# A hybrid decoder block on one core: the last store of the gate matrix, some row gathers and the first expert group's gate in another order

## Chip, cores and metric

One Trainium2 chip, one core. The metric is the device time of one execution in microseconds (us); the median of several runs is compared. Engines: PE is the matmul engine (TensorE), DVE is VectorE, ACT is ScalarE, POOL is GpSimd, SP is the engine that issues most transfers (DMAs).

## The reference, cut to what matters

One decoder block on 512 tokens of width 2048: pooling and latent attention, then a product-key expert layer, then a gated embedding. The change lies in the expert layer:

```python
def peer_ffn(xn, wq, sub_keys, u, v):
    q = (xt @ wq).reshape(t, PEER_HEADS, 2, PEER_HALF_DIM)
    sc = jnp.einsum('thpc,hpnc->thpn', q, sub_keys)
    top_v, top_i = lax.top_k(sc, PEER_TOPK)
    ...                                  # 16 best of the 256 pairs, for each of 8 heads
    gate = jax.nn.softmax(best_v, axis=-1)
    hc = jnp.einsum('cd,chkd->chk', xc, u[ec])      # u, v: 16384 x 2048
    ac = gc * jax.nn.gelu(hc)
    out = jnp.einsum('chk,chkd->cd', ac, v[ec])
```

## The kernel before

Tokens lie along the free axis, features along the partitions. Every weight unit (16 blocks of 128 by 128) is loaded as two halves of 512 KB into `raw`, split by ACT into a rounded part `w_hi` (`hi`, L1155) and by DVE into the rest `w_lo` (`lo`, L1643), and multiplied by PE in three passes of 16 blocks, 48 matmuls in a unit. `raw` is one buffer of two halves: a half is loaded again only when its `lo` is done (`load_unit`, L509).

The expert layer computes 342 of the 512 tokens densely, against all 16384 experts, with a gate matrix (expert by token) that is zero but for the chosen pairs. The other 170 tokens are done row by row: POOL gathers one row of u or v for each of 128 partitions (1 MB, `load_row`, L2483), DVE multiplies and sums it (L2045).

Before the groups the gate matrix is made in DRAM. For the first 128 dense tokens POOL scatters single gates (`put_gate_of`: 8 heads with 16 puts each; the first put of a head waits until all puts of the heads before have landed). For the other tokens DVE makes one-hot vectors in 27 sets, PE multiplies them, ACT evicts them into `g_blk` and SP stores seven blocks; of the last one (L583, 256 KB) the part that the first groups need goes first and the remaining 1792 KB follow (L604). While this runs, PE computes u units that are spilled, and DVE takes ten `early_row` dots at fixed places between the sets; with two buffers, the gather of an early row waits for the dot two rows before. POOL issues the gathers of early rows 2 to 9 between the sixteen puts of the last head: two puts, one gather, and so on (L2531 to L2534).

Then come 32 groups of 4 times 128 experts. A group is three u units (k = 0 to 2) and four v units (k = 3 to 6). The gate path of one of its four blocks is a chain of small instructions: DVE `scale`, ACT `gelu`, DVE `gate`, ACT `gated_hi`, DVE `gated_lo`. ACT's `between(k, j, a)` puts the conversion of the halves of unit k around gelu and gated_hi; DVE's `chain` does the same for `lo`. Each engine works in the order written.

Group 0 is special (`first=True`). Its units still use `raw`. SP loads the halves of k = 3, then issues `load_g` for group 1 (the gate tile, L610, and the spilled products, L613), then loads k = 4 to 6. ACT evicts the second set of token rows into `x_rows_b` (`rows_evict_b`, L1474) between k = 3 and k = 4; that tile lies over `g_blk`, so the first eviction waits until all stores of the blocks have landed:

```python
if i == 0:
    act.wait_ge(g_stored[0], 16 * ((ONE_TB + 1) // 2))      # L1477
```

Behind it on ACT stand the second eviction, two `rows_stage_b` (16 small copies), and then the conversion of k = 4. DVE's second `gated_lo` into the next group waits for the same count. POOL starts the gathers of the groups' rows when the stores and the second half of k = 3 have landed; group 0 has three rows, the later ones 10 or 11. Below, v0, v1, v2, v3 are the v units of group 0 (k = 3 to 6).

## Time and profile before

| | us |
|---|---|
| runs before: median of 3 | 2986.7 |
| lowest and highest of them | 2975.47, 2995.12 |
| the profiled execution | 2986.3 |
| its span, first to last instruction | 2984.5 |
| PE busy in the span | 2946.4 |

The profile is of one execution. 1.8 us of its time lie outside the span. A transfer's time to landing runs from its issue to the completion. The granted clock is 1.00 at full speed (2.4 GHz) and 0.50 at half (1.2 GHz).

### The profile page before, as it was taken

Reading aid. Unit: us, or ns where it says so; the run is one execution under the profiler, and the core shown is the slowest. Engines: PE = TensorE matmul, PEld = TensorE weight load, DVE = VectorE, ACT = ScalarE, POOL = GpSimd, SP = SyncE. Lnnn points to the kernel's source line nnn. Section 1 sums busy time; section 2 is a strip of 40 time slices with the busy share of each in tenths; the row PEclk is TensorE's granted clock in tenths of the full one; section 3 lists DMA queues with packets and bytes.
Section 4 is the critical chain, followed back from the end, with each engine's and each line's share of the span. In section 5 each row is a group of like instructions: output and inputs, shape, how many; then the busy total and the mean of one; then the engine's idle time right before and its main releaser. Section 6 shows DMA issues by size and latency. Waiting matters only on the chain.

```text
span 2984.5 us, 45570 instructions
## 1 busy us (share of the span) xinstructions
PE 2946.4 (99%) x17422; PEld 2746.1 (92%) x17422; DVE 2459.3 (82%) x3694; ACT 1057.9 (35%) x1433; POOL 775.4 (26%) x519
## 2 busy tenths in 40 slices
PE   9999999999999999999999999999999999999998
PEld 7777778888999999999999999999999999999887
DVE  7544443479998969999999999999999999998745
ACT  5224332232234653323333333333333333334522
POOL 0120000027776202222222222323333333230000
PEclk9999999999999999999999999999999999999999
DMA  4242222345557889999999999999999999995322
GB/s 170 91 160 98 84 71 98 112 121 143 144 125 220 301 289 361 349 357 382 360 376 359 364 385 365 375 375 367 373 367 377 359 370 372 372 366 184 107 98 100
DMA packets 209496, 779.52 MB, mean 261 GB/s; under 512 B 50561, under 2 KB 104065, under 8 KB 135041
## 3 DMA queue, kind: packets, MB, share of 16 engines
q1 hardware_dynamic: 136784, 413.90, 38.3%
q0 software_dynamic: 67680, 358.71, 33.0%
q10 hardware_dynamic: 4944, 5.81, 0.6%
q8 instruction: 47, 0.77, 0.1%
q14 instruction: 41, 0.33, 0.0%
HBM read 745.22 MB, written 33.10 MB: 261 GB/s over the span
## 4 chain that ended last, share of the span: by engine, by line
PE 75%; DVE 13%; DMA 4%; SPq 3%; issue 3%; POOL 1%; ACT 1%; DVEq 0%; ACTq 0%; POOLq 0%
PE bank L656 23%; PE bank L657 23%; PE bank L658 23%; DVE w_lo L1656 2%; DMA raw_whole<-in_u_t 2%; SPq L613 2%; DVE row L2045 2%; POOL gate_matrix L2478 1%; PE bank L747 1%; DVE w_lo L1643 1%; PE bank L770 1%; PE bank L748 1%; DVE h L2231 1%; DMA raw_whole<-in_v_t 1%; DVE one_g L2093 1%
## 5 line engine op out<-in xcount | busy, mean ns | idle before, releaser
L656 PE MATMUL bank<-x_hi,w_hi 128*128 128x342 f32 (+2 forms) x2912 | 1001.1, 344 | 11.6 <-DVE w_lo L1643 5.0
L657 PE MATMUL bank<-x_lo,w_hi 128*128 128x342 f32 (+2 forms) x2912 | 997.3, 342 | 0.0
L658 PE MATMUL bank<-x_hi,w_lo 128*128 128x342 f32 (+2 forms) x2912 | 991.0, 340 | 0.0
L656 PE MATMUL bank<-a_hi,w_hi 128*128 128x342 f32 x2048 | 654.1, 319 | 7.1 <-DVE a_lo L2146 2.5
L658 PE MATMUL bank<-a_hi,w_lo 128*128 128x342 f32 x2048 | 652.0, 318 | 0.0
L657 PE MATMUL bank<-a_lo,w_hi 128*128 128x342 f32 x2048 | 649.7, 317 | 0.0
L656 PEld LDWEIGHTS bank<-x_hi,w_hi 128*128 128x128 f32 x2912 | 549.6, 189 | 54.5 <-DVE w_lo L1656 6.7
L657 PEld LDWEIGHTS bank<-x_lo,w_hi 128*128 128x128 f32 x2912 | 548.3, 188 | 37.1 <-issue 1.2
L658 PEld LDWEIGHTS bank<-x_hi,w_lo 128*128 128x128 f32 x2912 | 548.4, 188 | 37.0
L656 PEld LDWEIGHTS bank<-a_hi,w_hi 128*128 128x128 f32 x2048 | 387.0, 189 | 14.8 <-issue 9.2
L657 PEld LDWEIGHTS bank<-a_lo,w_hi 128*128 128x128 f32 x2048 | 387.3, 189 | 0.0
L658 PEld LDWEIGHTS bank<-a_hi,w_lo 128*128 128x128 f32 x2048 | 386.8, 189 | 0.0
L1175 ACT ACTIVATE w_hi<-raw_whole 128x1024 fp32r<-128x1024 f32 x216 | 223.0, 1053 | 452.0 <-DMA raw_whole<-in_u_t 196.6
L1175 ACT ACTIVATE w_hi<-raw_b_whole 128x1024 fp32r<-128x1024 f32 x216 | 223.0, 1053 | 443.4 <-DMA raw_b_whole<-in_u_t 187.6
L2497 POOL DMA_INDIRECT row<-in_v,expert x128 | 205.6, 1607 | 478.3 <-DVE x_rows L2058 286.8
L2478 POOL DMA_INDIRECT gate_matrix<-put_gate,cell x128 | 233.9, 1827 | 338.2 <-DVE cell L1982 289.8
L1643 DVE TENSOR_TENSOR w_lo<-raw_whole,w_hi 128x1024 fp32r<-128x1024 f32 (+1 forms) x218 | 256.8, 1204 | 64.5 <-ACT w_hi L1162 60.9
L2058 DVE SCALAR_TENSOR_TENSOR x_rows<-row,mix,x_rows 128x2048 f32<-128x2048 f32 x127 | 297.6, 2343 | 0.0
L2497 POOL DMA_INDIRECT row<-in_u_rows,expert x113 | 152.5, 1349 | 519.3 <-DVE row L2045 456.7
L1656 DVE TENSOR_TENSOR w_lo<-raw_whole,w_hi 128x1024 fp32r<-128x1024 f32 x216 | 263.2, 1219 | 23.9 <-ACT w_hi L1175 23.8
L1656 DVE TENSOR_TENSOR w_lo<-raw_b_whole,w_hi 128x1024 fp32r<-128x1024 f32 x216 | 263.1, 1218 | 19.4 <-ACT w_hi L1175 19.4
L1162 ACT ACTIVATE w_hi<-raw_whole 128x1024 fp32r<-128x1024 f32 (+1 forms) x218 | 217.5, 1030 | 172.5 <-PE bank L658 51.6
(271 smaller groups left out, 3174.2 us busy)
## 6 DMA issues: line engine op xcount, KB each, us to landing
raw_whole<-in_v_t SPq DMA_DIRECT2D x62, 1024.0 KB, 7.6
raw_b_whole<-in_v_t SPq DMA_DIRECT2D x62, 1024.0 KB, 8.1
raw_b_whole<-in_u_t SPq DMA_DIRECT2D x46, 1024.0 KB, 9.2
raw_whole<-in_u_t SPq DMA_DIRECT2D x46, 1024.0 KB, 8.8
raw_whole<-in_u_t SPq DMA_DIRECT2D x72, 512.0 KB, 4.1
beside<-gate_matrix SPq DMA_DIRECT2D x31, 704.0 KB, 15.4
raw_whole<-in_w_o SPq DMA_DIRECT2D x32, 512.0 KB, 3.9
raw_whole<-in_w_q SPq DMA_DIRECT2D x32, 512.0 KB, 3.8
```

The source lines that it names most:

```text
L613: sp.dma_start(h_pre[par][:, :, :], by_quarters(h_dram[g])).then_inc(h_in[par], 16)
L656: pe.matmul(out, w_hi[slot][:, blk, :], m_hi, start=first, stop=False)
L657: pe.matmul(out, w_hi[slot][:, blk, :], m_lo, start=False, stop=False)
L658: return pe.matmul(out, w_lo[slot][:, blk, :], m_hi, start=False, stop=last)
L1162: act.activation(w_hi[slot][:, 8 * s:8 * s + n, :], raw[s][:, 0:n, :], ACT.Copy)\
L1175: act.activation(w_hi[slot][:, 8 * s:8 * s + 8, :], raw_two[x][s][:, :, :], ACT.Copy).then_inc(hi_ready, 1)
L1643: dve.tensor_tensor(w_lo[slot][:, 8 * s:8 * s + n, :], raw[s][:, 0:n, :], w_hi[slot][:, 8 * s:8 * s + n, :].bitcast(F32), ALU.subtract)\
L1656: dve.tensor_tensor(w_lo[slot][:, 8 * s:8 * s + 8, :], raw_two[x][s][:, :, :], w_hi[slot][:, 8 * s:8 * s + 8, :].bitcast(F32), ALU.subtrac ...
L2045: dve.scalar_tensor_tensor(got[:, :], got[:, :], 1.0, (x_rows_b if part_b else x_rows)[:, :], ALU.mult, ALU.mult, accum_out=column(dots_b ...
L2058: dve.scalar_tensor_tensor(to[:, :], row[b][:, :], column(mix_b if part_b else mix, k), to[:, :], ALU.mult, ALU.add).then_inc(row_done, 1)
L2478: pool.indirect_dma_start(g_dram.rearrange("b j i t -> (b j i t)").unsqueeze(1), bass.IndirectOffsetOnAxis(ap=cell[:, hd, k:k + 1], axis=0 ...
L2497: pool.indirect_dma_start(into[:, :], None, table, bass.IndirectOffsetOnAxis(ap=index, axis=0))\
```

## The change

Four edits. (1) On SP the rest of the last block is no longer stored before the waits ahead of group 0 but inside group 0, behind the loads of v0 and `load_g` for group 1. (2) On ACT and DVE, in group 0 only, the gate of block p+2 is done whole before v0 is converted, instead of around it. (3) On POOL the gathers of group 0 and 1 get waits of their own: row 0 for v0's second half (as before), row 1 for v1's first half, row 2 for all stores and v1's second half, group 1's first row for v2's first half. (4) On POOL the gathers of early rows 2 and 3 go ahead of the last head's first puts; of its puts, 12 then stand between the gathers and 4 behind the last.

```diff
--- before.py
+++ after.py
@@ -601,7 +601,6 @@
             for b in range(stored, ONE_TB):
                 store_block(b, b % 2)
             load_unit(U_PEER + 3, packed(u_t, GROUP))
-            sp.dma_start(g_dram[N_TB - 1, :, TOPK:NK, :], g_blk[(ONE_TB - 1) % 2][:, TOPK:NK, :]).then_inc(g_stored[0], 16)
             sp.wait_ge(g_stored[1], 16 * (ONE_TB // 2))
             sp.wait_ge(g_first, 16)
             sp.wait_ge(spill_stored, 16 * N_GROUPS)
@@ -627,6 +626,9 @@
                         sp.dma_start(pt[:, :, :], p_t).then_inc(p_in, 16)
                     if first and q == 0:
                         load_g(g + 1, 1 - par)
+                    if first and q == 0:
+                        sp.dma_start(g_dram[N_TB - 1, :, TOPK:NK, :], g_blk[(ONE_TB - 1) % 2][:, TOPK:NK, :])\
+                            .then_inc(g_stored[0], 16)
 
             peer_group(0, 0, first=True)
             sp.wait_ge(g_stored[0], 16 * ((ONE_TB + 1) // 2))
@@ -1533,7 +1535,11 @@
                 if last:
                     activate(p + 2, a_slot(2, par))
                 else:
-                    between(3, p + 2, a_slot(2, par))
+                    if first:
+                        activate(p + 2, a_slot(2, par))
+                        hi_peer(g, 3, par, first=True)
+                    else:
+                        between(3, p + 2, a_slot(2, par))
                     if first:
                         rows_evict_b(0)
                         rows_evict_b(1)
@@ -2210,6 +2216,14 @@
                     scale(p + 2, 2, par, g2, peer_unit(g, 1), (2 + par) % 2)
                     gate(p + 2, 2, par, g2)
                     gated_lo(p + 2, 2, par)
+                elif first:
+                    scale(p + 2, 2, par, g2, peer_unit(g, 1), (2 + par) % 2)
+                    gate(p + 2, 2, par, g2)
+                    gated_lo(p + 2, 2, par)
+                    rows(3)
+                    lo_half(3, 0)
+                    lo_half(3, 1)
+                    rows(4)
                 else:
                     chain(p + 2, 2, par, g2, 3, 3, peer_unit(g, 1), (2 + par) % 2)
                     rows(4)
@@ -2506,6 +2520,16 @@
                     else:
                         k = first_b(g) + b_places(g).index(n)
                         index = expert_b[:, k:k + 1]
+                    if g == 0 and n == 0:
+                        pool.wait_ge(raw_loaded[1], 16 * (peer_unit(0, 3) + 1))
+                    if g == 0 and n == 1:
+                        pool.wait_ge(raw_loaded[0], 16 * (peer_unit(0, 4) + 1))
+                    if g == 0 and n == 2:
+                        for s in range(2):
+                            pool.wait_ge(g_stored[s], 16 * ((ONE_TB + 1 - s) // 2))
+                        pool.wait_ge(raw_loaded[1], 16 * (peer_unit(0, 4) + 1))
+                    if g == 1 and n == 0:
+                        pool.wait_ge(raw_loaded[0], 16 * (peer_unit(0, 5) + 1))
                     load_row(first_place(g) + n, index, table)
 
             pool.wait_ge(zeros_stored, 16 * 2 * PUT_TB)
@@ -2528,18 +2552,17 @@
                         load_row(TOP)
                     if hd == PH - 2 and k == TOPK // 2 + 2:
                         load_row(TOP + 1)
-            for k in range(2, EARLY):
+            load_row(TOP + 2)
+            load_row(TOP + 3)
+            for k in range(4, EARLY):
                 for j in range(2):
-                    put_gate_of(PH - 1, 2 * k - 4 + j)
+                    put_gate_of(PH - 1, 2 * k - 8 + j)
                 load_row(TOP + k)
-            for k in range(2 * EARLY - 4, TOPK):
+            for k in range(2 * EARLY - 8, TOPK):
                 put_gate_of(PH - 1, k)
             pool.wait_ge(row_done, FRONT)
             pool.wait_ge(g_done, 2 * N_OH)
-            for s in range(2):
-                pool.wait_ge(g_stored[s], 16 * ((ONE_TB + 1 - s) // 2))
             pool.wait_ge(expert_b_in, 16 * 2 * SHARE)
-            pool.wait_ge(raw_loaded[1], 16 * (peer_unit(0, 3) + 1))
             for g in range(G_DOT):
                 load_group(g, u_rows)
             for g in range(G_DOT, N_GROUPS - 1):
```

## Rows read from the trace of the kernel before

**Rows 1.** The page: engines over the span, and the group of the puts.

```profile
PE 2946.4 (99%) x17422; PEld 2746.1 (92%) x17422; DVE 2459.3 (82%) x3694; ACT 1057.9 (35%) x1433; POOL 775.4 (26%) x519
...
L2478 POOL DMA_INDIRECT gate_matrix<-put_gate,cell x128 | 233.9, 1827 | 338.2 <-DVE cell L1982 289.8
```

**Rows 2.** Windows: PE, PEld, DVE, ACT, POOL busy (x instructions), clock, DMA share, GB/s.

```profile
1000.00:1062.00 62.00, 61.95 (x587) 59.87 (x585) 59.11 (x70) 41.93 (x46) 7.44 (x4) 1.00 0.74 275
...
1171.00:1330.00 159.00, 153.65 (x970) 151.14 (x969) 147.20 (x180) 52.35 (x66) 43.05 (x31) 1.00 0.95 360
1913.00:1966.00 53.00, 53.00 (x341) 52.95 (x340) 52.31 (x52) 17.62 (x22) 18.23 (x11) 1.00 0.98 375
```

**Rows 3.** Waits of PE in 925 to 1000 us: us in total, times, longest.

```profile
PE bank L656 <- DVE x_lo L1643: 2.2, 2, 1.8
PE bank L949 <- DVE one_g L2093: 1.7, 2, 0.9
PE bank L949 <- ACT g_blk L1436: 0.4, 1, 0.4
PE bank L656 <- DVE w_lo L1643: 0.3, 1, 0.3
```

**Rows 4.** The chain of waits, 918 to 938 us (start us, us, what).

```profile
918.97 6.20 DMA gate_matrix<-put_gate,cell
...
929.99 7.99 DMA early_row<-in_u_rows,expert
```

**Rows 5.** Timeline of DVE, the same stretch (start us, us, what, idle before).

```profile
930.93 1.23 DVE L1643 TENSOR_TENSOR x_lo<-raw_whole,x_hi 128x1024 fp32r<-128x1024 f32 x1 [0.32 <-ACT x_hi L1162]
938.00 2.29 DVE L2045 SCALAR_TENSOR_TENSOR early_row<-early_row,x_rows 128x2048 f32<-128x2048 f32 x1 [5.84 <-DMA early_row<-in_u_rows,expert]
```

**Rows 6.** Transfers, five stretches: count, KB each, median us to landing.

```profile
raw_whole<-in_u_t SPq DMA_DIRECT2D x3, 512.0 KB, 3.4
...
raw_whole<-in_u_t SPq DMA_DIRECT2D x1, 512.0 KB, 7.3
...
gate_matrix<-g_blk SPq DMA_DIRECT2D x1, 2048.0 KB, 8.9
...
gate_matrix<-g_blk SPq DMA_DIRECT2D x1, 1792.0 KB, 10.2
...
beside<-spilled_scores SPq DMA_DIRECT2D x1, 176.0 KB, 8.3
```

**Rows 7.** Timeline of the SP queue around group 0.

```profile
1071.67 0.43 SPq L604 DMA_DIRECT2D gate_matrix<-g_blk  x1
...
1081.34 0.44 SPq L610 DMA_DIRECT2D beside<-gate_matrix  x1
1081.82 0.65 SPq L613 DMA_DIRECT2D beside<-spilled_scores  x1
```

**Rows 8.** Wait of PE in 1080 to 1120 us (as rows 3).

```profile
PE bank L656 <- DVE a_lo L2146: 2.5, 1, 2.5
```

**Rows 9.** Timeline of ACT in group 0.

```profile
1088.85 1.07 ACT L1479 ACTIVATE x_rows_b<-bank 128x512 f32<-128x512 f32 x2
...
1093.62 1.05 ACT L1162 ACTIVATE w_hi<-raw_whole 128x1024 fp32r<-128x1024 f32 x1
1094.57 0.49 ACT L1483 ACTIVATE beside<-h_s 128x352 f32<-128x352 f32 x1
```

**Rows 10.** Windows in group 0 (columns as rows 2).

```profile
1091.00:1096.00 5.00, 5.00 (x24) 5.00 (x23) 1.30 (x2) 4.06 (x14) 1.81 (x2) 0.66 0.91 328
1096.00:1103.00 7.00, 6.58 (x46) 6.35 (x45) 4.22 (x8) 2.53 (x4) 0.00 (x0) 1.00 1.01 401
```

**Rows 11.** The chain of waits into the third v unit.

```profile
1107.62 1.07 ACT w_hi L1162
...
1108.71 1.24 DVE w_lo L1643
...
1110.04 0.39 PE bank L656
```

## Prediction

> **What bounds the kernel now.** I read the page first: PE is busy 99% of the span [rows 1], so an edit pays only by idle or half-clock time of PE that it removes, and costs only what it adds of these. The windows over the expert groups say how much there is. A full group window of 53 us holds 341 matmuls, 0.155 us each, so a unit of 48 takes 7.5 us. Groups 1 to 3 hold 970 in 159 us where 1023 would fit: 53 are missing, 8.2 us, and the transfers are busy 95% of that time [rows 2]. So PE is the bound in late groups, and any shift of PE's work before them reaches the end, unless these 8.2 us of stalls change with it.
>
> Then I asked for PE's waits around the two places that the diff touches. Between 925 and 1000 us PE waits 4.6 us in six pieces, nearly all for DVE [rows 3]. The chain of waits tells what held DVE: POOL's put waits 6.2 us for the puts of the heads before, then come two puts, then an early row's gather takes 8.0 us [rows 4], and DVE stands still for 5.84 us before that row's dot [rows 5]. After 1000 us, with DVE busy for 59.1 of 62 us, PE is busy for 61.95: no stall is left there [rows 2]. In group 0 PE waits 2.5 us for `a_lo`, the gate of block p+2 [rows 8]; a little later its clock is at the lower level, 1.2 GHz, for a time: 0.66 of full speed over 5 us, 1.7 us lost [rows 10].
>
> **Edit 4, early rows 2 and 3 ahead of the puts.** The put that waits at 918.97 for 6.2 us is the first of the last head; in that time POOL does nothing. The gather of early row 2 needs only a dot that is done, so it is issued about 922, after the put that starts at 918.97, and not at 929.99; with the same 8.0 us it lands at 930, before DVE comes to it at 932.1 [rows 4, 5]. DVE's 5.84 us of idling would go. What may take their place is the half that DVE splits just before, at 930.93, whose conversion it waited for by 0.32 us [rows 5]. Halves of this stretch land in 3.4 us; one that ran beside a gather and puts took 7.3 [rows 6]. Now two gathers (2.1 MB) run beside it. Ends: not slowed, 5.84 us of lead for DVE; slowed by 3.9 us, some 2 us of lead. I take a half of about 5 us, 1.6 late, and 4.3 us of lead, since the two gathers share the transfer engines with little else. The stalls are 4.6 us in all [rows 3] and are served by the lead one after another, so the gain is the smaller of the two: **−4.3 us**, bounds −2.0 and −4.6. The later early gathers keep their waits on dots and move with DVE. Four puts, at 1.8 us each [rows 1], now follow the last gather. SP needs all puts landed only before group 0's first gate tile, some 30 us on, so they cost nothing; without that cover it would be up to 4 × 1.8 us plus the 6.2 us wait of rows 4.
>
> **Edit 2, the gate of p+2 ahead of v0.** Its work is the same, in another order: no instruction more or less. `a_lo` comes before v0's halves have landed, and what PE waits for is v0's second `w_lo`, 2.4 us after its conversion starts (1.09 + 1.24 + the start, as in [rows 11]). The wait of 2.5 us shrinks, at best to nothing; I take a shrinkage of 1.4 us, and the clock stays up. Those 1.4 + 1.7 us are gained only if v1 is ready when v0 ends. It is not, by the next step, so here I cost it at 0.
>
> **Edit 1, the store behind v0 and the gate tile.** SP issued it at 1071.67; now it comes after L613, which is issued from 1081.82 to 1082.47 [rows 7]. It adds nothing to SP's queue but its issue of 0.43 us. The wait that counts is ACT's at L1477: the first eviction into `x_rows_b`. Before, the store had landed at 1071.67 + 10.2 = 1081.9 [rows 6, 7] and the eviction ran at 1088.85 with no wait. Now it runs when the store lands; call that S. Queued behind it on ACT are the second eviction, two stagings and v1's conversion, which began 4.8 us after the first eviction [rows 9]; who waits for them is DVE's `lo` of v1 and with it PE. From the start of v1's conversion to PE's start on v1 I count 4.5 us: 1.1 to the first `lo`, 1.2 for it, 0.9 for one addition and the gate product between the two `lo` on DVE, 1.3 for the second `lo` and the start (durations from [rows 9, 11]). So v1 starts at S + 9.3.
>
> S, from below: the fastest of the block stores shown took 8.9 us from issue, although 2048 KB [rows 6]: 1082.5 + 8.9 = 1091.4. From above: what stands ahead in the queue, the spilled products, lands at 1081.82 + 8.3 = 1090.1 [rows 6, 7]; if the store's 1.84 MB and row 0's gather of 1.05 MB, which POOL issues at about 1087, then share 401 GB/s [rows 10], it is 2.89 / 0.401 = 7.2 us more: 1097.3. I take 1096.0, nearer to the upper end, because the queue is not empty as it was at 1071.67: 0.9 MB of small pieces are ahead. v1's own halves are issued from 1087 on, behind the store, and need 2.6 us of the same rate; they land before ACT comes to them at S + 4.8.
>
> The Trainium skill, DMA: Bandwidth & Descriptors, section "Queues, rings and completion order", says that each transfer engine consumes one queue in order and alternates between queues by packets. This trace agrees as far as it goes: the spilled products, issued last, land last of that set. By the rule the whole gather could be served between the store's packets, which is the upper end, 1097.3, and would make the sum 1.3 us larger.
>
> PE's side: v1 starts at 1105.3. v0 now ends near 1097, so PE idles about 8 us. An idling of 2.5 us was followed by the 1.7 us of half clock above [rows 8, 10], so I add 1.7 for this longer one. v1 takes 7.5, and v2 starts at S + 9.3 + 7.5 + 1.7 = S + 18.5 = 1114.5. Before it started at 1110.04 [rows 11]. From there on the order is as before. **Cost: S − 1091.5 = +4.5 us.** Bounds: with S at 1091.4 and no clock loss −1.8; with S at 1097.3 +5.8, and +7.5 if the half clock lasts twice as long.
>
> **Edit 3, the gathers' waits.** Row 0 goes no later than before. Rows 1 and 2 leave v1's and the store's way and land about 1108, group 1's first row about 1120. DVE multiplies the three rows at the starts of v1, v2 and v3 and the fourth in group 1, after 1125, so the slack is 5 us or more: 0. If this cover went, DVE would wait for one row, up to about 5 us.
>
> **Sum.** 2986.3 (the profiled execution) − 4.3 + 0 + 4.5 + 0 = 2986.5, span 2984.7. The median of the runs is 0.4 above the profiled execution, so 2986.9, rounded to **2987 us**.
>
> **Rivals.**
> - *The early store (faster).* S is at 1092 or less because the store's large pieces overlap the small ones ahead. Then v1 is ready when PE is nearly done with v0, edit 2's gain counts and the clock stays up: −1.8 − 4.3 = 2980.2. Against it: 0.9 MB ahead in the queue. It begins to win as S falls under 1092.
> - *The late store (slower).* S at 1097.3 and a longer half clock: +7.5 − 4.3, 2989.5, and with edit 4's lead at its lower bound 2991.8. It decides as soon as S is later than 1095.8, where edit 1 costs more than edit 4 gives. For it: transfers are busy 91 to 101% of this time [rows 10].
> - *The first groups' stalls move.* 8.2 us are lost in groups 1 to 3 for late transfers [rows 2]; another spacing of the gathers there could remove most of it: −7.5, 2979. Against it: from group 1's second row on the gathers wait for DVE's dots, in both kernels.
> - *No effect.* The half before early row 2 is as late as it can be (+2.3 against the sum), and the delay of group 0 is taken back in the groups' stalls (−4.5): about 2984.
>
> **Chances.** Forecast (2984.5 to 2989) 0.35, early store 0.15, late store 0.25, stalls move 0.15, no effect 0.10. All five lie within 8 us of the sum. The three runs of before spread over 19.7 us, so a median may be 5 us or more off. The range is 2979 to 2991.8 widened by about 4 us to each side: **2975 to 2996**. The forecast's own range is 2982 to 2992. About 1%, 30 us, is what a measurement of this kernel can tell from no change; no case reaches it. Faster by over 1% 0.02, within 1% 0.97, slower by over 1% 0.01.
>
> **What would show it.** Edit 4 is right if DVE's 5.84 us before the early row at 938 are gone and PE's six waits before 1000 with them, and group 0 starts 4 us earlier. Edit 1 is right if ACT idles before the first L1479 until the store lands, 13 to 14 us after its issue, and PE then waits about 8 us for v1's `w_lo` with the clock at half for a while. Edit 2 is right if the wait for `a_lo` is replaced by a shorter one for `w_lo`. The forecast is wrong if the store lands in under 10 us, or if the matmuls missing in groups 1 to 3 are not 50 or so again.

## The result, and the profile after

The changed kernel takes 2991.4 us (median of 22 runs, 2982.9 to 3002.5) where the kernel before takes 2984.7 on the same chips (22 runs, 2975.5 to 2995.3). The ratio is 1.0020, with a 95% interval of 1.0012 to 1.0029: slower by 0.2%, 6 us, and within 1%. The forecast was 2987 in a range of 2975 to 2996, a change of 0.2 us and within 1%. The profiled execution of the changed kernel took 2991.1 us, its span is 2989.3.

In the changed kernel's profile line numbers are 2 to 14 higher than before: the matmuls are L658 to L660, `lo` is L1649, `hi` L1164, the eviction L1481, the late store L630, `load_g` L609 and L612, a row's dot L2051, its gather L2511.

The page: the engines over the span, and the group of the puts. PE is busy for the same time as before [rows 1]; the 4.8 us that this span has more than the 2984.5 before are idling of PE.

```profile
PE 2946.3 (99%) x17422; PEld 2747.1 (92%) x17422; DVE 2459.2 (82%) x3694; ACT 1058.2 (35%) x1433; POOL 794.4 (27%) x519
...
L2492 POOL DMA_INDIRECT gate_matrix<-put_gate,cell x128 | 233.4, 1823 | 334.4 <-DVE cell L1988 289.8
```

**Edit 4, the early rows.** PE's waits from 925 to 1000 us (answer to [rows 3]) are 2.5 us instead of 4.6:

```profile
PE bank L658 <- DVE w_lo L1649: 1.3, 2, 1.0
PE bank L658 <- DVE x_lo L1649: 0.8, 1, 0.8
PE bank L951 <- ACT g_blk L1438: 0.4, 1, 0.4
```

The chain of waits and DVE's timeline of the same stretch (answers to [rows 4, 5]):

```profile
924.20 7.83 DMA raw_whole<-in_u_t
```

```profile
933.15 1.23 DVE L1649 TENSOR_TENSOR w_lo<-raw_whole,w_hi 128x1024 fp32r<-128x1024 f32 x1 [1.77 <-ACT w_hi L1164]
935.79 1.23 DVE L1649 TENSOR_TENSOR x_lo<-raw_whole,x_hi 128x1024 fp32r<-128x1024 f32 x1 [1.42 <-ACT x_hi L1164]
936.94 2.28 DVE L2051 SCALAR_TENSOR_TENSOR early_row<-early_row,x_rows 128x2048 f32<-128x2048 f32 x1
```

The early row is there in time: its dot at 936.94 has no idling ahead of it, where there were 5.84 us. But it starts only 1.1 us earlier than before (938.00), because DVE splits two halves ahead of it, waits for each (1.77 and 1.42 us), and the first of them landed 7.83 us after its issue. Group 0's gate tile is issued at 1063.12 instead of 1064.17.

**Edit 1, the store.** The queue of SP (answer to [rows 7]), ACT (answer to [rows 9]) and the chain of waits (answer to [rows 11]):

```profile
1080.69 0.43 SPq L609 DMA_DIRECT2D beside<-gate_matrix  x1
1081.17 1.13 SPq L612 DMA_DIRECT2D beside<-spilled_scores  x1
1082.34 2.49 SPq L630 DMA_DIRECT2D gate_matrix<-g_blk  x1
```

```profile
1093.54 1.09 ACT L1481 ACTIVATE x_rows_b<-bank 128x512 f32<-128x512 f32 x2 [6.62 <-DMA gate_matrix<-g_blk]
...
1098.32 1.04 ACT L1164 ACTIVATE w_hi<-raw_whole 128x1024 fp32r<-128x1024 f32 x1
```

```profile
1082.34 11.13 DMA gate_matrix<-g_blk
...
1112.20 9.66 DMA raw_whole<-in_v_t
...
1124.31 0.63 PE bank L658
```

The store is issued at 1082.34 and lands at 1093.5, the moment S of the prediction. ACT idles 6.62 us for it, and v1's conversion starts at S + 4.8. PE's waits from 1092 to 1130 us (answer to [rows 8]):

```profile
PE bank L658 <- DVE w_lo L1649: 7.9, 2, 4.3
PE bank L908 <- ACT stage_b L1429: 1.8, 2, 1.3
```

The waits come in three places: 1.8 us for `stage_b` and 3.6 us for v1's `w_lo`, both behind the eviction, and then 4.3 us, in one piece, for v3's. Ahead of them, at v0, PE waits 1.2 us for `w_lo` where it waited 2.5 us for `a_lo`, and the clock stays up (1.00 from 1087 to 1093.5, where 1091 to 1096 before had 0.66). The kernel before waits at v1 and v2 too: beside the line of [rows 8] its waits of 1080 to 1120 have a second one, 0.4 us at v1 and 1.5 us at v2.

```profile
PE bank L656 <- DVE w_lo L1643: 1.9, 2, 1.5
```

The wait for v3 is the one that the prediction had no term for. Its half is the 9.66 us of the chain above. A load of 1 MB of group 1's u, issued at 1112.65, ran beside it, and POOL's timeline shows what else did, three gathers of 1 MB:

```profile
1108.54 0.94 POOL L2511 DMA_INDIRECT row<-in_u_rows,expert  x1 [8.38 <-DMA raw_whole<-in_v_t]
1109.78 1.65 POOL L2511 DMA_INDIRECT row<-in_u_rows,expert  x1 [0.30 <-issue]
1115.49 0.94 POOL L2511 DMA_INDIRECT row<-in_u_rows,expert  x1 [4.06 <-DVE row L2051]
```

Windows of the changed kernel (columns as in [rows 2]; the last one answers a row there). The clock after each of the two idle stretches is at its lower level, and in 1072 to 1080 the transfer engines are busy for a fifth of the time:

```profile
1072.00:1080.00 8.00, 8.00 (x52) 7.99 (x52) 4.94 (x8) 4.85 (x8) 0.00 (x0) 1.00 0.21 80
```

```profile
1100.00:1107.00 7.00, 4.29 (x15) 4.32 (x16) 6.52 (x10) 2.17 (x4) 0.16 (x1) 0.51 0.96 343
1124.00:1128.00 4.00, 3.69 (x15) 3.73 (x16) 4.00 (x7) 2.01 (x2) 0.00 (x0) 0.58 0.73 242
1171.00:1330.00 159.00, 157.77 (x1005) 156.68 (x1004) 152.63 (x186) 53.19 (x66) 43.83 (x33) 1.00 0.97 371
```

The kernel before, the first of these windows:

```profile
1072.00:1080.00 8.00, 8.00 (x55) 8.00 (x54) 4.30 (x8) 5.58 (x8) 0.00 (x0) 1.00 0.89 308
```

This pair is the heart of the case. Before, the 1792 KB of the store filled a stretch in which nobody else wanted the transfer engines (share 0.89), and it had landed 7 us before ACT asked for it. After, that stretch is empty (0.21) and the store stands where v0's and v1's halves and a row's gather are wanted.

**Where the 6 us come from.** Group 0 starts 1.0 us earlier. v2 starts at 1112.3 instead of 1110.04, 2.3 us later. v3 starts at 1124.3 instead of 1117.7, 6.6 us later, and then loses some 1.6 us at the half clock (4 us at 0.58). The gate tile of group 3 is issued 8.0 us later than before (1178.09 against 1170.13), that of group 4 only 5.2 us later (1230.89 against 1225.67). From 1171 to 1330 PE does 1005 matmuls instead of 970 [rows 2]; at 0.155 us the 35 are 5.4 us, which leaves a delay of 2.6 us at 1330. The span ends 4.8 us later, so about 2 us are lost again behind it.

Whether the 5.4 us are group 0's delay taken back isn't shown. In the 160 us from 110 us after group 0's gate tile (two windows of each profile, added) the kernel before does 978 matmuls and the changed one 1013, but the twelve kernels below do 993 to 1026, those too whose group 0 isn't late (x1_early_rows 1026, x4_store_back 1016). The profiled execution of the kernel before stalls more there than any other.

### The profile page after: what moved, and what is told of

Its sections match the earlier page's. It is cut to its first block, busy times and chain, and to the rows that moved or that the text cites. A ratio compares the mean times of both kernels' runs of the same rounds, so it can differ in the third digit from the quotient of the medians.

```text
span 2989.3 us, 45570 instructions
## 1 busy us (share of the span) xinstructions
PE 2946.3 (99%) x17422; PEld 2747.1 (92%) x17422; DVE 2459.2 (82%) x3694; ACT 1058.2 (35%) x1433; POOL 794.4 (27%) x519
## 4 chain that ended last, share of the span: by engine, by line
PE 60%; DVE 23%; DMA 8%; SPq 4%; issue 3%; ACT 2%; DVEq 0%; ACTq 0%
PE bank L658 18%; PE bank L659 18%; PE bank L660 18%; DVE w_lo L1662 6%; DVE row L2051 5%; DMA raw_whole<-in_u_t 4%; SPq L612 3%; DMA raw_b_whole<-in_u_t 2%; DVE h L2245 2%; DVE w_lo L1649 1%; DVE x_rows L2064 1%; PE bank L749 1%; DMA raw_whole<-in_v_t 1%; PE bank L772 1%; PE bank L750 1%
## 5 line engine op out<-in xcount | busy, mean ns | idle before, releaser
L658 PE MATMUL bank<-x_hi,w_hi 128*128 128x342 f32 (+2 forms) x2912 | 1001.5, 344 | 13.0 <-DVE w_lo L1649 6.6
L660 PE MATMUL bank<-x_hi,w_lo 128*128 128x342 f32 (+2 forms) x2912 | 990.7, 340 | 0.0
L658 PE MATMUL bank<-a_hi,w_hi 128*128 128x342 f32 x2048 | 654.3, 319 | 11.7 <-DVE w_lo L1649 9.1
L660 PE MATMUL bank<-a_hi,w_lo 128*128 128x342 f32 x2048 | 652.6, 319 | 0.0
L658 PEld LDWEIGHTS bank<-x_hi,w_hi 128*128 128x128 f32 x2912 | 549.6, 189 | 56.5 <-DVE w_lo L1662 5.2
L660 PEld LDWEIGHTS bank<-x_hi,w_lo 128*128 128x128 f32 x2912 | 548.4, 188 | 37.2
L658 PEld LDWEIGHTS bank<-a_hi,w_hi 128*128 128x128 f32 x2048 | 387.7, 189 | 17.6 <-DVE w_lo L1649 8.6
L660 PEld LDWEIGHTS bank<-a_hi,w_lo 128*128 128x128 f32 x2048 | 387.5, 189 | 0.0
L1177 ACT ACTIVATE w_hi<-raw_b_whole 128x1024 fp32r<-128x1024 f32 x216 | 223.1, 1054 | 439.4 <-PE bank L660 197.6
L2511 POOL DMA_INDIRECT row<-in_v,expert x128 | 217.1, 1696 | 455.9 <-DVE x_rows L2064 270.7
L1649 DVE TENSOR_TENSOR w_lo<-raw_whole,w_hi 128x1024 fp32r<-128x1024 f32 (+1 forms) x218 | 256.8, 1204 | 72.8 <-ACT w_hi L1164 69.2
L2511 POOL DMA_INDIRECT row<-in_u_rows,expert x113 | 152.5, 1349 | 516.9 <-DVE row L2051 446.0
L1164 ACT ACTIVATE w_hi<-raw_whole 128x1024 fp32r<-128x1024 f32 (+1 forms) x218 | 217.4, 1030 | 170.9 <-PE bank L660 51.5
```

The source lines that it names most:

```text
L658: pe.matmul(out, w_hi[slot][:, blk, :], m_hi, start=first, stop=False)
L660: return pe.matmul(out, w_lo[slot][:, blk, :], m_hi, start=False, stop=last)
L1164: act.activation(w_hi[slot][:, 8 * s:8 * s + n, :], raw[s][:, 0:n, :], ACT.Copy)\
L1177: act.activation(w_hi[slot][:, 8 * s:8 * s + 8, :], raw_two[x][s][:, :, :], ACT.Copy).then_inc(hi_ready, 1)
L1649: dve.tensor_tensor(w_lo[slot][:, 8 * s:8 * s + n, :], raw[s][:, 0:n, :], w_hi[slot][:, 8 * s:8 * s + n, :].bitcast(F32), ALU.subtract)\
L2511: pool.indirect_dma_start(into[:, :], None, table, bass.IndirectOffsetOnAxis(ap=index, axis=0))\
```

## The experiments

Twelve kernels ran, each timed against the kernel before in five rounds. Single runs of one kernel spread over some 15 us, and a profiled execution can stand far off its kernel's median (z2_group1_rows_later 12 us above it, x2_store 9 us below). The medians come from several chips, on which the kernel before took 2984.2 to 2988.1, so they are not compared with one another. For time I use the ratios, for mechanism the stretches of a profile: when group 0's gate tile is issued (called tile 0), and how many matmuls PE does in the 170 us from there, summed from six windows (a matmul on the border of two counts in both, in every kernel).

| kernel | edits | median us | ratio, 95% interval | tile 0 at | matmuls in 170 us |
|---|---|---|---|---|---|
| before | none | 2984.7 | 1 | 1064.17 | 1044 |
| x1_early_rows | 4 | 2980.1 | 0.9996, 0.9984 to 1.0007 | 1063.72 | 1071 |
| x2_store | 1 | 2990.9 | 1.0032, 1.0022 to 1.0041 | 1063.98 | 1010 |
| x3_no_gather_waits | 1, 2, 4, two waits of 3 | 2987.6 | 1.0009, 0.9998 to 1.0021 | 1063.52 | 1028 |
| x4_store_back | 2, 3, 4 | 2986.3 | 1.0006, 0.9994 to 1.0019 | 1062.62 | 1055 |
| x5_gate_order | 2 | 2985.1 | 1.0000, 0.9988 to 1.0013 | 1066.45 | 1063 |
| x6_one_row | half of 4 | 2981.4 | 0.9994, 0.9983 to 1.0005 | 1061.14 | 1060 |
| x7_gather_waits | 3 | 2987.9 | 1.0013, 1.0001 to 1.0024 | 1064.47 | 1054 |
| y1_tile_early | 2, 4, tile early | 2983.8 | 0.9993, 0.9979 to 1.0006 | 1063.15 | 1055 |
| y2_tile_early_store_late | all, tile early | 2986.8 | 1.0005, 0.9993 to 1.0018 | 1066.13 | 1005 |
| z1_one_row_gate | 2, half of 4 | 2985.0 | 0.9997, 0.9983 to 1.0011 | 1065.34 | 1073 |
| z2_group1_rows_later | all, one wait later | 2992.2 | 1.0027, 1.0017 to 1.0036 | 1065.38 | 1006 |
| z3_store_first | all, store ahead of tile | 2996.4 | 1.0029, 1.0017 to 1.0041 | 1064.07 | 1014 |
| the changed kernel | all | 2991.4 | 1.0020, 1.0012 to 1.0029 | 1063.12 | 999 |

The last column parts the table in two. The eight kernels that store early do 1044 to 1073 matmuls (mean 1059), the six that store late 999 to 1028 (mean 1010). The 49 matmuls between, at 0.155 us, are 7.6 us. The stretch from tile 0 to the third gate tile (group 2's) parts the same way: 51.5 to 54.6 us in the eight (mean 52.7), 56.8 to 61.5 us in the six (mean 59.3). So a late store makes group 0 some 6.6 us longer, whatever the other edits are. By the ratios of the whole kernels these six take 1.5 to 9.5 us more than the kernel before, the others from 2.1 less to 3.9 more.

**Edit 4 alone (x1_early_rows).**

```diff
-            for k in range(2, EARLY):
+            load_row(TOP + 2)
+            load_row(TOP + 3)
+            for k in range(4, EARLY):
                 for j in range(2):
-                    put_gate_of(PH - 1, 2 * k - 4 + j)
+                    put_gate_of(PH - 1, 2 * k - 8 + j)
                 load_row(TOP + k)
```

> The kernel before with only the fourth edit: the gathers of early rows 2 and 3 ahead of the last head's puts. Theory A (the gathers slow the weight halves beside them, so DVE's wait moves rather than goes): DVE's wait of 5.84 us before the early row is replaced by waits of 1 to 2 us for conversions, the gate tile of group 0 is issued 1 to 2.5 us earlier than before, and the time is 1 to 2.5 us less than before, about 0.05%. Theory B (my sum on record): 4.3 us less. Theory C (the edit is worth nothing, the later puts take it back): 0.

Its chain of waits: the half beside the two gathers, and the early row's dot right behind it.

```profile
927.00 8.15 DMA raw_whole<-in_u_t
...
936.27 1.23 DVE x_lo L1643
937.49 2.21 DVE early_row L2045 x2
```

The dot starts at 937.49 instead of 938.00. The wait did not go, it moved from the row to the half: DVE now waits 5.1 us for that half's conversion. The same shows in all eight kernels with edit 4: the half beside the two gathers takes 7.8 to 8.8 us in every profile. The ratio, 0.9996, can't be told from 1.

**Only early row 2 ahead of the puts (x6_one_row)**, to see whether the second gather is what stretches the half.

```diff
+            load_row(TOP + 2)
+            for k in range(3, EARLY):
                 for j in range(2):
-                    put_gate_of(PH - 1, 2 * k - 4 + j)
+                    put_gate_of(PH - 1, 2 * k - 6 + j)
```

> The kernel before with half of the fourth edit: only early row 2's gather goes ahead of the last head's puts, row 3 stays between them; 2 puts follow the last gather. Theory A (two gathers at once, 2 MB, hold up the weight half beside them, 8.2 us instead of 3.4): with one gather the half lands within 6 us, DVE waits 1 to 3 us less there than with two, and group 0's gate tile is issued 1 to 3 us earlier than before, 1 to 3 us less time than before. Theory B (any gather there does it): the same as the fourth edit alone, 0 to 1 us.

```profile
927.01 5.69 DMA raw_whole<-in_u_t
```

The half took 5.69 us instead of 8.15, DVE's longest wait there was 2.6 us, and group 0's tile was issued 3.0 us earlier than before. So it looked settled. But the same order of POOL's work ran once more in another kernel.

**One early row and edit 2 (z1_one_row_gate)**, the two pieces that looked free or useful.

> The kernel before with only early row 2 gathered ahead of the last head's puts (row 3 stays behind its two puts) and with the gate of p+2 whole before v0 is converted. Theory A (the two pieces that paid when alone add up): group 0's gate tile is issued 2.5 to 3.5 us earlier than before's 1064.17, and the stretch from it to the third tile is 51.5 to 53 us against 53.85; ratio to before 0.9980 to 0.9992. Theory B (what comes early is taken back by the late transfers of groups 1 to 3): group 0 starts early, yet the ratio is 0.9994 to 1.0003.

```profile
931.46 8.79 DMA raw_whole<-in_u_t
```

This is not the half of x6_one_row but the next one. DVE's timeline of z1_one_row_gate around the early row's dot:

```profile
934.23 2.29 DVE L2049 SCALAR_TENSOR_TENSOR early_row<-early_row,x_rows 128x2048 f32<-128x2048 f32 x1
...
941.36 1.23 DVE L1647 TENSOR_TENSOR x_lo<-raw_whole,x_hi 128x1024 fp32r<-128x1024 f32 x1 [4.84 <-ACT x_hi L1162]
```

The dot starts at 934.23, 0.7 us earlier than in x6_one_row (934.96). But the next half, issued at 931.46 beside row 3's gather and puts, takes 8.79 us where it took 4.7 in x6_one_row, DVE waits 4.84 us for it, and tile 0 comes at 1065.34. The order of work up to that point is that of x6_one_row, so two executions of one order differ by 4.2 us, and the 3.0 us above were partly luck. What the profiles do support is a mean: tile 0 is issued at 1064.8 on average in the four kernels without edit 4 (1063.98 to 1066.45), at 1064.0 in the eight with it (1062.62 to 1066.13), and at 1061.1 and 1065.3 in the two with half of it. By these means edit 4 is worth about 0.8 us, less than two executions of one order differ, so it isn't told from nothing. Of the expectations, theory A's group stretch came (51.5 us from tile 0 to the third tile), its early start did not, and the ratio of 0.9997 is B's, with an interval that holds both.

**Edit 2 alone (x5_gate_order).** The two hunks of the diff in ACT's and DVE's group 0, nothing else.

> The kernel before with only the second edit: in group 0 the gate of block p+2 is done whole before v0 is converted. Theory A (v0's second half lands last, so what PE waits for turns from a_lo into w_lo with nearly the same end): the wait before v0 goes from 2.5 us to about 2, the time is within 1.5 us of before. Theory B (the gate was what held v0): the wait before v0 falls to 0.5 us or less and the half clock behind it goes, 3 to 4 us faster.

PE's waits from 1080 to 1130 us, and a window:

```profile
PE bank L656 <- DVE w_lo L1647: 4.8, 3, 2.4
```

```profile
1085.00:1095.00 10.00, 8.23 (x53) 7.97 (x52) 3.94 (x5) 7.52 (x22) 3.85 (x4) 1.00 0.85 270
```

The wait for `a_lo` [rows 8] is gone, v0 waits 1.8 us for its own `w_lo`, and the clock stays at 1.00 where it was 0.66 [rows 10]. v1 then waits more for its own halves, and the ratio is 1.0000. This is the cost of 0 that the prediction gave it, for the reason that it gave.

**Edit 1 alone (x2_store).**

```diff
-            sp.dma_start(g_dram[N_TB - 1, :, TOPK:NK, :], g_blk[(ONE_TB - 1) % 2][:, TOPK:NK, :])...
...
                     if first and q == 0:
                         load_g(g + 1, 1 - par)
+                    if first and q == 0:
+                        sp.dma_start(g_dram[N_TB - 1, :, TOPK:NK, :], ...)
```

> The kernel before with only the first edit: the rest of the last block stored behind v0 and the gate tile; the gathers of group 0 all wait for that store, as the old wait says. Theory A (ACT's first eviction waits for the store, and v1 starts 9.2 us after it lands; what comes on top in the changed kernel is from the gathers' waits): ACT idles until the store lands at about 1094, v1 starts at 1103 to 1105, PE waits 3 us or more there with half clock behind it, and the time is 3 to 6 us more than before. Theory B (the store alone carries the whole loss of the changed kernel and more, since edits 2 to 4 help): 7 us or more slower than before. Theory C (the store is free): within 1 us of before.

```profile
PE bank L658 <- DVE w_lo L1645: 6.9, 3, 3.4
PE bank L658 <- DVE a_lo L2148: 2.0, 1, 2.0
```

This is the dearest part: 1.0032, +9.5 us (6.6 to 12.2), theory B's time, while v1 starts at 1103.8 as theory A has it. The store took 10.97 us and ACT waited 5.51 us for it. In this kernel POOL's old wait holds every gather until the stores have landed, so four gathers of 1 MB are issued in 3.8 us from 1095.43 on. Of the 6.9 us, v1 waits 3.4, behind the store; v2 and v3 wait 2.1 and 1.4 us for halves beside the gathers, which take 9.00 and 6.70 us in the chain.

**Everything but edit 1 (x4_store_back).**

> The changed kernel with only the first edit undone: the store stands where it stood before, the gate order, the gathers' waits and the early rows are the changed ones. Theory A (the store's place delays ACT's eviction and v1; the spacing of the gathers delays v3): no wait of ACT for the store, v1 starts at 1096 to 1098 with at most 1 us of waiting, v3 waits 0 to 4 us; 3 to 8 us faster than the changed kernel, so 0 to 3 us faster than before. Theory B (the gathers' spacing alone is the loss): v3 still waits 4 us or more and the time stays within 2 us of the changed kernel.

The eviction runs at 1087.76 with no wait, PE waits 4.8 us in three pieces from 1080 to 1130 (4.4 us before), and the ratio falls from 1.0020 to 1.0006; the two intervals overlap, 1.0012 being below 1.0019. One of the pieces is 1.2 us at v3, where before had none. From both sides the store's place costs 4 us (with the others, at the edge of what the ratios tell) to 9.5 us (alone, clear of it).

**The changed kernel without the new spacing of the gathers (x3_no_gather_waits).** Of the waits in `load_group` only row 0's and row 2's wait for the stores stay.

```diff
-                    if g == 0 and n == 1:
-                        pool.wait_ge(raw_loaded[0], 16 * (peer_unit(0, 4) + 1))
...
-                        pool.wait_ge(raw_loaded[1], 16 * (peer_unit(0, 4) + 1))
-                    if g == 1 and n == 0:
-                        pool.wait_ge(raw_loaded[0], 16 * (peer_unit(0, 5) + 1))
```

> The changed kernel without the third edit's spacing: row 0 waits for v0's second half and row 2 for the stores, but row 1, row 2 and group 1's first row wait for no v unit. Theory A (v3 was late in the changed kernel because group 1's first gathers were released in its transfer): PE's wait of 4.3 us before v3 goes or falls under 1.5 us; in exchange two gathers run beside the store, it lands 1 to 3 us later and v1 starts that much later; in sum 0 to 4 us faster than the changed kernel. Theory B (the spacing protects v1 and v2 and costs nothing): 2 us or more slower than the changed kernel, with new waits before v1 or v2 and v3's wait unchanged.

The chain, v1's second half, and PE's waits from 1092 to 1130:

```profile
1089.53 13.42 DMA raw_whole<-in_v_t
```

```profile
PE bank L658 <- DVE w_lo L1649: 4.5, 1, 4.5
PE bank L908 <- ACT stage_b L1429: 2.2, 2, 1.2
```

Rows 0 and 1 are now gathered at 1088.0 and 1089.4, beside the store, and v1's second half takes 13.42 us. v1 waits more, v3 not at all, as theory A has it, and the whole is 1.0009 where the changed kernel is 1.0020. The intervals overlap; the matmuls (1028 against 999, one profile each) point the same way. So it looks as if edit 3's spacing, behind a late store, costs rather than saves, but that isn't shown.

**Edit 3 alone (x7_gather_waits).**

> The kernel before with the gathers' new waits alone (edit 3); store, gate and early rows as before. Theory A (the spacing moves the gathers from v1's and v2's halves onto v3's, whatever the store does): PE waits 1 to 4 us for v3's w_lo, where before has none from 1114 on, the stretch from group 0's gate tile to the third tile is 54.5 to 57 us against 53.85, ratio 1.0003 to 1.0012. Theory B (the spacing costs only behind a late store): no wait at v3, stretch 52 to 54.2 us, ratio 0.9993 to 1.0003.

PE's waits from 1104 to 1130:

```profile
PE bank L656 <- DVE w_lo L1643: 1.5, 2, 1.3
```

v3 waits 1.3 us where before had no wait from 1114 on, as theory A has it, and the ratio, 1.0013 with 1.0001 to 1.0024, is A's upper end. But the stretch from tile 0 to the third tile is 52.5 us, as theory B has it, and 1054 matmuls are no fewer than in x4_store_back or y1_tile_early. The shift onto v3 is real and small: with an early store the two kernels with edit 3 wait there (1.3 us here, 1.2 in x4_store_back), the six without it don't. That edit 3 alone slows the kernel is at the edge of what was measured, and these stages don't show where.

**Group 1's first rows gathered later (z2_group1_rows_later)**, a direct trial of what holds v3's half.

```diff
                     if g == 1 and n == 0:
-                        pool.wait_ge(raw_loaded[0], 16 * (peer_unit(0, 5) + 1))
+                        pool.wait_ge(raw_loaded[1], 16 * (peer_unit(0, 6) + 1))
```

> The changed kernel, with one wait altered: the first row of group 1 is gathered when v3's second half has landed, and not when v2's first half has. Nothing is left out. Theory A (v3 waits because its second half runs beside the gathers released at 1108.5 and 1109.8): the half lands in 5 to 7 us and not 9.7, PE's wait for v3's w_lo falls from 4.3 us to under 1.5, the stretch from group 0's gate tile to the third tile falls from 61.5 us to 56 to 58.5, ratio 1.0003 to 1.0012. Theory B (the half is held by the 1 MB load of u and by row 2's gather, which stay): the wait stays at 3 us or more, the stretch at 60 us or more, ratio 1.0015 to 1.0027.

The chain of waits from 1114 on, and ACT's waits from 1114 to 1180:

```profile
1114.90 4.53 DMA raw_whole<-in_v_t
...
1121.80 10.86 DMA raw_whole<-in_u_t
1135.04 11.00 DMA raw_b_whole<-in_u_t
```

```profile
ACT w_hi L1177 <- DMA raw_whole<-in_u_t: 11.7, 2, 6.2
ACT w_hi L1177 <- DMA raw_b_whole<-in_u_t: 10.1, 1, 10.1
```

The mechanism is theory A's: with the gathers away the half lands in 4.53 us instead of 9.66, though the 1 MB load of u is issued right behind it as before (1115.35), and PE's wait for v3 is gone (none from 1114 to 1130). The stretch to the third tile is 56.8 us, in A's range. But the time isn't: 1.0027, B's upper end, not better than the changed kernel. The gathers now run beside group 1's u loads, which take 10.86 and 11.00 us, and ACT waits over 21 us for them. In this execution the store also took 13.24 us, and PE waited 9.2 us in 1340 to 1860 against 3.2 in the changed kernel. But this execution, 3003.9 us, is the slowest of the kernel's eleven (median 2992.2), so its late waits don't stand for the others; what costs the time is open. In this profile the wait was moved once more, to group 1's loads of u: from 1130 to 1340 PE waits 3.3 us for `w_lo`, 0.9 in the changed kernel.

**The gate tile ahead of v0's loads (y1_tile_early, y2_tile_early_store_late).** This uses the idle transfer engines of 1072 to 1080. y1 keeps the old store and edits 2 and 4; y2 is the changed kernel.

```diff
-                    if first and q == 0:
-                        load_g(g + 1, 1 - par)
...
+            load_g(1, 1)
             peer_group(0, 0, first=True)
```

> The kernel before with the second and fourth edits, and with the gate tile and spilled products of group 1 issued behind the rest store and ahead of v0's loads, at about 1072 to 1073 instead of 1081. Theory A (v0's halves are slowed by the tile's small pieces issued right behind them): v0's second half lands in about 4.5 us instead of 6.5, the wait before v0 is 0.5 us or less with no half clock behind it, group 0 is 2 to 4 us shorter, 2 to 5 us faster than before. Theory B (the transfers are in one line, so what goes ahead of v0 delays it by as much): within 1.5 us of before.

> The changed kernel with the gate tile and spilled products of group 1 issued ahead of v0's loads, so that the rest store goes right behind v0 and lands earlier. Theory A (v1 starts 9.2 us after the store lands): the store lands at about 1090 to 1091 instead of 1093.5, v1 starts 9.2 us after that, 2 to 3 us earlier than in the changed kernel, and v3 still waits 2 to 4 us for its second half, released with the gathers; 2 to 4 us faster than the changed kernel. Theory B (the store's landing is not what v1 waits for): v1 starts at the same time as in the changed kernel.

In y1 v0 still waits 1.9 us for its `w_lo`, so the small pieces weren't what held v0's halves; 0.9993, which can't be told from 1. In y2 the window shows the gap filled, and the chain the store and v3's half:

```profile
1072.00:1080.00 8.00, 7.08 (x48) 6.83 (x47) 3.61 (x6) 6.25 (x14) 0.00 (x0) 1.00 0.95 278
```

```profile
1084.50 10.01 DMA gate_matrix<-g_blk
...
1111.82 10.98 DMA raw_whole<-in_v_t
```

With nothing small ahead the store lands 10.0 us after its issue, 28.4 us after tile 0 instead of 30.4, and ACT waits 3.34 us for it. v1 starts 9.3 us after it, as theory A has it. The ratio is 1.0005 against 1.0020, 4.5 us better with intervals that overlap, although v3's wait is still there (5.0 us). It may recover much of what the late store costs, not more than that.

**The store ahead of the gate tile (z3_store_first)**, the other way to have less ahead of it.

```diff
                     if first and q == 0:
-                        load_g(g + 1, 1 - par)
+                        sp.dma_start(g_dram[N_TB - 1, :, TOPK:NK, :], ...)
                     if first and q == 0:
-                        sp.dma_start(g_dram[N_TB - 1, :, TOPK:NK, :], ...)
+                        load_g(g + 1, 1 - par)
```

> The changed kernel with the store behind v0's loads but ahead of group 1's gate tile and spilled products. Nothing is left out. Theory A (the 0.9 MB of small pieces ahead of the store are what stretches it from 10.2 us to 11.1): the store lands 8.9 to 10.2 us after its issue, which is itself 1.6 us earlier, so it lands 26.5 to 28.5 us after group 0's gate tile is issued (30.4 in the changed kernel), PE's waits for v1 fall from 5.4 us to 1.5 to 3.5, ratio 1.0006 to 1.0015. Theory B (what shares the engines with it, v0's last halves before and row 0's gather and the small pieces after, holds it wherever it stands): it lands 10.8 us or more after its issue, 28.6 or more after the tile, PE's waits for v1 stay at 4 us or more, ratio 1.0013 to 1.0024.

ACT's first eviction, the chain of waits, and PE's waits from 1092 to 1130:

```profile
1091.07 1.08 ACT L1481 ACTIVATE x_rows_b<-bank 128x512 f32<-128x512 f32 x2 [3.38 <-DMA gate_matrix<-g_blk]
```

```profile
1086.93 10.48 DMA raw_whole<-in_v_t
```

```profile
PE bank L658 <- DVE w_lo L1649: 7.9, 3, 4.2
```

The store's part is as theory A expected: issued at 1081.26, landed 9.8 us later (1091.07), 27.0 us after tile 0. But the rest isn't: v1 still waits 4.2 us, now for its own half, which takes 10.48 us behind the small pieces and beside row 0's gather, v2 waits 3.5 us more, and the ratio is 1.0029, above what both theories gave, with an interval (1.0017 to 1.0041) that holds theory B's upper part. Here clearing the way for the store handed the lateness to the next transfer in the queue. The prediction's claim that v1's halves land before ACT comes to them holds only because ACT comes late.

## Why the prediction was right where it was, and where it was not

The total was right, 2987 against 2991.4, with the right class, and the range held. Much of that is the width of the range, 21 us for a kernel whose single runs spread as far: as a change, 0.2 us was forecast and 6.0 came, and the interval of 3.6 to 8.7 doesn't hold the forecast. The sum was made of two terms that nearly cancel; edit 4's was well off, the store's by 1.4 us, and a zero was wrong. By its own last sign the forecast failed: of the 1023 matmuls that fit into 1171 to 1330, 18 are missing and not about 50.

- *Edit 4, −4.3 us.* The steps "the gather is issued about 922" (920.3 was measured) and "DVE's 5.84 us of idling would go" held. The term that was mis-sized is the half ahead of the row, "about 5 us, 1.6 late": it took 7.83 us, and 8.15 in the kernel with this edit alone. The prediction had the row for it, the 7.3 us of a half beside a gather and puts [rows 6], and argued it away because the two gathers "share the transfer engines with little else". It also read one row amiss: the put that starts at 918.97 is the last of the head before, and POOL works on it for 3.05 of the 6.2 us; the first put of the last head starts at 925.92. The gather's place behind the put of 918.97 is right all the same. The dot came 0.5 to 1.1 us earlier in these two kernels, not 4.3, and tile 0 by 0.8 on average, less than the bound of 2.0. The timing by ratio, 0.9996 with 0.9984 to 1.0007, is 1.2 us of gain and doesn't exclude more.
- *Edit 2, 0.* Right, alone (1.0000), and by its own reason: in x5_gate_order v0's wait is shorter and the half clock is gone, and PE then waits 2.4 us for v1, where it waited 0.4. Its sign came too, 1.2 us for `w_lo` in place of 2.5 for `a_lo`. With the late store it may be worth more; that wasn't parted from edit 4.
- *Edit 1, S − 1091.5.* The formula held: v1 started at S + 9.2 (9.3 forecast), v2 at 1112.3 where S + 18.5 gives 1112.0. S itself was 1093.5, which is 1094.6 on the prediction's scale, where edit 4's shift of 1.05 is counted apart; 1096.0 was forecast. The small pieces landed 7.2 us after their issue, not 8.3, and from 1087 to 1093.5 the engines moved 421 GB/s, not 401. So the term is +3.1 and not +4.5. S fell between the early store's limit of 1092 and the late store's of 1095.8, so neither of these rivals came. The store landed 11.1 us after its issue, not 13 to 14, and PE idled 5.4 us there, not about 8. The half clock held for nearly all of 1100 to 1107 (0.51) and cost about 2 us of v1, where 1.7 was set.
- *The queues.* From the rule of the Trainium skill, DMA: Bandwidth & Descriptors, section "Queues, rings and completion order", that an engine takes its queues in turns by packets, the prediction derived that a whole gather may be served between the store's packets, S = 1097.3. That end wasn't reached: row 0's gather, issued at 1086.67, landed 10.2 us later, at 1096.9, 3.4 us after the store. That engines take one queue in order, as that section of the Trainium skill has it, agrees with v1's half, issued behind the store at 1086.94, which also landed 10.2 us later.
- *Edit 3, 0.* The step that failed. The prediction asked only whether each row is there when DVE wants it, with 5 us of slack, and that was so: no row was waited for. It didn't ask what the later gathers run beside. They ran beside v3's halves: 4.3 us of wait and 1.6 of half clock. z2_group1_rows_later shows that cause directly (the half lands in 4.53 us without them), x3_no_gather_waits that without the spacing v3 doesn't wait, but v1 waits longer.
- *"From there on the order is as before."* It wasn't, for the same reason: v3 came 6.6 us late where v2 was 2.3 late.
- *The first groups' stalls.* The prediction set 970 matmuls in 1171 to 1330, and 1005 ran: 5.4 of the 8.2 us of stalls weren't there. The sum has no term for that. Since every other profile too has fewer stalls there than that of the kernel before, the 970 belong in part to that one execution, and no rival that rests on the 8.2 us can be judged from them.

Put together from the profiled executions: v2 starts 2.3 us late (3.1 for the store, 1.05 less for the early start), v3 4.3 more, the clock 1.6, and about 3 are gone by group 4's tile: 5.2 us there, 4.8 at the span's end, 6.0 (3.6 to 8.7) by the runs. That the two profiles differ by about what the runs do is partly luck, since each may stand some us off its median. The prediction had 0.2. It credited edit 4 with 3.3 us too much, charged the store 1.4 too much, and left out 5.9 us at v3 and the 3 that came back.

What is settled: the store's new place is the main cause. Done alone it slows the kernel beyond the interval (1.0032, 1.0022 to 1.0041), and in all six kernels that have it group 0 is longer than in any of the eight that don't; that undoing it in the changed kernel gives 1.0006 agrees, with an interval that overlaps. And v3's wait comes from the gathers beside its half. What stays open: how much edit 3 costs by itself, why removing v3's wait (z2_group1_rows_later) doesn't make the kernel faster, how much of a delay of group 0 the next groups take back, and whether any version beats the kernel before. x1_early_rows, x6_one_row and y1_tile_early stand at 0.9993 to 0.9996, and every interval holds 1.

## What to carry to other kernels

When a transfer is moved, look at the transfer engines' share in the place that it leaves as well as in the place where it goes: the store filled a gap (0.89 there, 0.21 without it) and held nobody up, and behind the gap it delayed what was wanted next. A delay of a gather isn't free because its row is still in time; find the load that it now runs beside, and whether that load has any slack. And where a stretch's transfers are all needed back to back, as here, reordering them can just move the wait from one unit to the next (row to half, v1 to v3, v3 to the next group's u), so count the bytes of the stretch before crediting a gain.

## What the runs showed of the hardware

In the kernel before a half of 512 KB issued at 926 with no gather on its way landed in 3.3 us; behind the gather of 929.99 the next half took 3.4 us and the one after it 7.1. With two gathers of 1 MB issued shortly before it took 7.8 to 8.8 us in eight profiles, with three gathers and a 1 MB load around it 9.7, beside two and a 1.8 MB store 13.4. One order of work gave 5.69 and 4.7 us for two halves in a row in one execution, and 4.7 and 8.79 in another. The length of an idling alone doesn't tell what the clock does: PE's idlings of 1.2 us (v0 in the changed kernel), 1.8 us and then 2.4 us (v0 and v1 in x5_gate_order) left the clock at 1.00, while one of 2.2 us in x4_store_back, one of 2.5 us before [rows 8, 10] and those of 3.6 us (with 1.8 just before) and 4.3 us in the changed kernel were followed by the lower level. The windows of x5_gate_order and x4_store_back with the 2.4 and the 2.2 us:

```profile
1095.00:1105.00 10.00, 7.58 (x52) 7.36 (x51) 5.55 (x9) 4.01 (x8) 0.03 (x1) 1.00 1.01 410
...
1085.00:1095.00 10.00, 7.75 (x41) 7.49 (x40) 4.28 (x5) 8.22 (x22) 2.03 (x2) 0.83 0.94 306
```
